# Entry of the even layer: norm weights by column, a projection of unscaled tokens, and an earlier state-space setup

## What is computed

```
x  = layer_norm(ALPHA*x + moe + ple, ln2_w, ln2_b)
hn = x * rsqrt(mean(x*x) + 1e-6) * norm_even_g      # rmsnorm
proj = hn @ w_in_even                               # q, k, v, u, z_a, z_b, 1024 columns each
# state-space model (s5) on u: per channel a complex recurrence
dt = exp(log_dt); mag = exp(lr*dt); ang = li*dt
a  = mag*(cos ang + i sin ang);  factors (a-1)/(lr+i li) scale B
x_t = a x_{t-1} + B u_t;  y_t = Re(C x_t) + D u_t   # run as phase turn, real scan, phase turn back
x  = x + concat(attention, glu(gelu(y))) @ w_out_even
```

## Time and profile before

| | us |
|---|---|
| median of three timed runs | 3200.54 |
| the profiled execution's own time | 3198.18 |
| its span | 3196.4 |
| PE busy | 3009.0 (94%) |
| DVE busy | 1547.4 (48%) |
| ACT busy | 837.8 (26%) |
| POOL busy | 283.5 (9%) |

### The profile page before, as it was taken

One profiled execution on the slowest core, in us unless ns is written; L12 is line 12 of the kernel. 1 busy time (PEld: TensorE's weight loads), 2 busy tenths in 40 slices (PEclk: granted clock), 3 DMA queues, 4 the chain that ended last, 5 costly groups with the idle time before them and its releaser, 6 DMA issues.

```text
span 3196.4 us, 42548 instructions
## 1 busy us (share of the span) xinstructions
PE 3009.0 (94%) x18244; PEld 2161.4 (68%) x18244; DVE 1547.4 (48%) x1846; ACT 837.8 (26%) x926; POOL 283.5 (9%) x260
## 2 busy tenths in 40 slices
PE   8999999899999999999999999879999998999898
PEld 6777777899977743333333333268858878998886
DVE  4465544674556522222222222357887554444765
ACT  3352221544434310110110110010000243444443
POOL 2042111000000000000000000035440000000100
PEclk9999988999998999999999999989999999999999
DMA  7543221446575599999999999843333355898543
GB/s 244 151 139 100 74 61 58 123 140 182 174 237 171 190 366 425 425 425 425 425 425 425 425 425 425 341 159 118 114 124 118 126 178 125 194 194 183 137 165 138
DMA packets 216144, 725.25 MB, mean 227 GB/s; under 512 B 16314, under 2 KB 18794, under 8 KB 165644
## 3 DMA queue, kind: packets, MB, share of 16 engines
q1 hardware_dynamic: 210716, 702.22, 62.6%
q0 software_dynamic: 4144, 18.14, 1.6%
q10 hardware_dynamic: 1088, 2.10, 0.2%
HBM read 720.28 MB, written 2.11 MB: 226 GB/s over the span
## 4 chain that ended last, share of the span: by engine, by line
PE 72%; DMA 12%; DVE 11%; ACT 4%; issue 1%; POOL 0%; DVEq 0%; ACTq 0%
PE psum L137 71%; DMA t<-in_w_up 12%; DVE t L283 8%; ACT t L254 2%; PE psum L143 2%; DVE t L294 1%; ACT t L256 1%; DVE t L298 1%; DVE t L306 0%; ACT L254 0%; POOL t L328 0%; DVE t L269 0%; ACT L256 0%; DMA t<-in_x 0%; DVE t L275 0%
## 5 line engine op out<-in xcount | busy, mean ns | idle before, releaser
L137 PE MATMUL psum<-t,t 128*128 128x256 f32 (+7 forms) x17166 | 2914.8, 379 | 135.3 <-DVE t L283 78.8
L137 PEld LDWEIGHTS psum<-t,t 128*128 128x128 f32 (+4 forms) x17166 | 2069.7, 175 | 941.2 <-issue 564.2
L283 DVE TENSOR_TENSOR t<-t,t 128x1024 fp32r<-128x1024 f32 (+6 forms) x642 | 786.0, 1224 | 495.8 <-ACT t L254 462.5
L254 ACT ACTIVATE t<-t 128x1024 fp32r<-128x1024 f32 (+8 forms) x521 | 528.6, 1015 | 901.4 <-PE psum L137 625.3
L283 DVE TENSOR_TENSOR t<-t,psum 128x1024 f32<-128x1024 f32 (+3 forms) x265 | 246.3, 929 | 741.3 <-PE psum L137 440.7
L254 ACT ACTIVATE t<-psum 128x1024 f32<-128x1024 f32 (+5 forms) x278 | 213.5, 768 | 1414.9 <-PE psum L137 1315.5
L328 POOL TENSOR_TENSOR t<-t,t 128x1024 f32<-128x1024 f32 (+8 forms) x133 | 222.9, 1676 | 571.7 <-DVE t L283 258.2
L283 DVE TENSOR_TENSOR t<-psum,t 128x1024 f32<-128x1024 f32 (+6 forms) x117 | 101.1, 864 | 121.9 <-PE psum L137 91.8
L143 PE MATMUL psum<-t,t 128*128 128x128 f32 (+1 forms) x566 | 87.9, 294 | 31.7 <-DVE t L294 18.0
L143 PEld LDWEIGHTS psum<-t,t 128*128 128x128 f32 (+1 forms) x566 | 67.6, 150 | 69.5 <-issue 39.8
L83 POOL DMA_DIRECT2D t<-in_s_lr x1 | 0.6, 574 | 1187.2 <-DVE t L306 1187.2
(11 more groups left out here) (67 smaller groups left out, 240.1 us busy)
## 6 DMA issues: line engine op xcount, KB each, us to landing
t<-in_w_gate SPq DMA_DIRECT2D x128, 1024.0 KB, 16.9
t<-in_w_up SPq DMA_DIRECT2D x128, 1024.0 KB, 18.4
t<-in_w_down SPq DMA_DIRECT2D x128, 1024.0 KB, 17.5
t<-in_w_in SPq DMA_DIRECT2D x160, 512.0 KB, 4.1
t<-in_w_in_odd SPq DMA_DIRECT2D x128, 512.0 KB, 5.4
t<-in_w_in_even SPq DMA_DIRECT2D x96, 512.0 KB, 3.8
t<-in_w_out SPq DMA_DIRECT2D x32, 512.0 KB, 4.3
t<-in_w_pg SPq DMA_DIRECT2D x32, 512.0 KB, 4.3
```

Of the source, the lines that this page charges most:

```text
L137: ins = self.e.matmul(o, l, r, start=start, stop=stop, skip_group_check=True)
L254: self.put(self.e.activation(o, i, f, scale=scale), event)
L283: self.put(self.e.tensor_tensor(o, a, b, op), event)
```

## The change

- **Norm by column.** DVE's second norm now only centres and scales each token (`centred`, one ts of 128x512 for each block and half, in place). Weight and bias are applied after PE's transposes, where a column is a partition: DVE (`gained`) writes `hTe` with weight and bias multiplied by the even gain (`l2g`), and ACT squares the same PSUM bank with weight and bias (`l2c`) into four buffers. Within a block DVE and ACT take turns on the two halves of the bank.
- **Unscaled projection.** PE starts u after half of the first block and puts the four sets of transposes between the pieces. POOL sums the squares (three tts of 128x1024, one of 128x512, one of 128x256), and PE forms `r1.sum` with one matmul after the eighth piece. DVE then makes the factor per token, scales u as it leaves PSUM (`states_in`, before a copy on ACT), and scales `hTe` in place, a quarter at a time, as soon as u has used it (`scaled_tokens`).
- **Earlier setup.** The small part of the state-space setup runs beside experts 8 to 10 on ACT and DVE; its loads (four DMAs) are issued in the experts too. After the meeting POOL has seven DMAs, then the powers, then the sum of squares, then the phases.
- **Residual rows later.** `x` gets `ln2_w` and `ln2_b` on POOL after phases 7: for each of two halves two broadcast loads of 512 KB, a wait, and four tts of 128x1024.
- **Layout and loads.** The experts' gather buffers move to the bottom of the memory so that six `w_in_even_2` pieces can land before the experts end; the two 1 MB loads of `ln2_w` and `ln2_b` on SP are gone.

The diff, cut to its core:

```diff
@@ tensor program, even()
+                def turned_pairs(j):
+                    w = pe.take("ev.T", j, of=(0, 3)).rearrange("p (k b t) -> p k b t", b=2, k=4)
+                    pe.wait_ge(("l2.x", j), j > 1 and ("ev.hTs", j - 2) or None)
+                    for k in range(4):
+                        for b in range(2):
+                            pe.tr(w[:, k, b, :], x[:, b, 512 * j + 128 * k:512 * j + 128 * k + 128],
+                                  event=("ev.T", j) if k == 3 and b else None)
+
+                turned_pairs(0)
+                for j in range(4):
+                    if j < 3:
+                        turned_pairs(j + 1)
+                    for i in (2 * j, 2 * j + 1):
+                        pe.wait_ge(("ev.hT", 2 * i + 1))
+                        some(first, 1)
+                ps = pe.take("r1.sum", of=(0, 3))
+                pe.wait_ge(("r1.squares",), ("ev.hTs", 3))
+                pe.mm(ps[:, 0:256], ones[:, 0:128], squares[0][:, 0, :], True, True, event=("r1.sum",))
                 some(first, 8)
-                rest = chain(native_b("ev.q", hTe, "w_in_even_2", 0, 1024, (0, 1)),
+
+                def queries():
+                    work = native_b("ev.q", hTe, "w_in_even_2", 0, 1024, (0, 1))
+                    for i in range(16):
+                        if i < 8:
+                            pe.wait_ge(("ev.hTn", i // 2))
+                        yield next(work)
@@ vector program: second_norm, the factor per token, the order
+
+                def centred(j):
                     for b in range(2):
-                        xc = x[:, b, cs]
-                        v.stt(xc, xc, mv[:, b, 0:1], l2w[:, cs], ALU.subtract, ALU.mult)
-                        v.stt(xc, xc, inv[:, b:b + 1], l2b[:, cs], ALU.mult, ALU.add, event=("l2.x", ci) if b else None)
-
-            def scaled_tokens():
-
-                v.wait_ge(("r1.sum", 3))
+                        xc = x[:, b, 512 * j:512 * j + 512]
+                        v.ts(xc, xc, mv[:, b, 0:1], inv[:, b:b + 1], ALU.subtract, ALU.mult,
+                             event=("l2.x", j) if b else None)
+
+                def gained(j):
+                    ps = v.bank("ev.T", j).rearrange("p (k b t) -> p k b t", b=2, k=4)
+                    v.wait_ge(("ev.T", j))
+                    for k in range(4):
+                        i = 4 * j + k
+                        if k == 2:
+                            v.wait_ge(("r1.square", j, 1))
+                        v.ts(hTe[:, i, :].rearrange("p (b t) -> p b t", b=2), ps[:, k], l2g[:, 0, i:i + 1],
+                             l2g[:, 1, i:i + 1], ALU.mult, ALU.add, event=("ev.hT", i))
+                    v.names(("ev.hTs", j))
+
+                centred(0)
+                centred(1)
+                v.wait_ge(("meet", "pe", 7), ("meet", "act", 7), ("meet", "pool", 7))
+                for j in range(4):
+                    gained(j)
+                    if j < 2:
+                        centred(j + 2)
...
+            def states_in(ci):
+                v.wait_ge(("ev.u", ci))
+                v.tt(uT[:, 4 * ci:4 * ci + 4, :], v.bank("ev.u", ci).rearrange("p (m t) -> p m t", m=4), over_tokens(4),
+                     ALU.mult, event=("ev.u.c", ci))
+                v.free("ev.u", ci)
+
+            def scaled_tokens(g4):
+                v.wait_ge(("used", "s", stream.turn + 9 + 2 * g4))
+                h4 = hTe[:, 4 * g4:4 * g4 + 4, :]
+                v.tt(h4, h4, over_tokens(4), ALU.mult, event=("ev.hTn", g4))
...
+                    if 8 <= ex < 11:
+                        (s5_decay, s5_angles, s5_factors)[ex - 8]()
...
                 s5_setup()
+                token_scales()
+                states_in(0)
+                for g4 in range(4):
+                    scaled_tokens(g4)
+                states_in(1)
                 s5()
@@ scalar program
+                    if ex == 8:
+                        a.wait_ge(("landed.s5a",))
+                        a.activation(dt, ld, ACT.Exp, event=("s5.dt",))
+                    elif ex == 9:
+                        a.wait_ge(("s5.lrdt",))
+                        a.activation(mag, mag, ACT.Exp, event=("s5.mag",))
+                    elif ex == 10:
+                        a.wait_ge(("s5.angles",))
+                        a.activation(sn, sn, ACT.Sin)
+                        a.activation(cs_, cs_, ACT.Sin, event=("s5.cos",))
...
+                ps = a.bank("ev.T", j).rearrange("p (k b t) -> p k b t", b=2, k=4)
+                a.wait_ge(("ev.T", j))
+                for k in (2, 3, 0, 1):
+                    i = 4 * j + k
+                    if k == 0:
+                        a.wait_ge(("ev.hT", i + 1))
+                    a.activation(squares[j][:, k, :].rearrange("p (b t) -> p b t", b=2), ps[:, k], ACT.Square,
+                                 bias=l2c[:, 1, i:i + 1], scale=l2c[:, 0, i:i + 1], event=("r1.square", j, k // 2))
                 a.free("ev.T", j)
@@ pool program
+            g.wait_ge(("mo.flagged",), ("pl.mul", 3))
+            g.load(("landed.s5a",), [(lr, I["s5_lr"]), (li, I["s5_li"]),
+                                     (ld[0:64, :], I["s5_ld"][0].partition_broadcast(64)),
+                                     (ld[64:128, :], I["s5_ld"][1].partition_broadcast(64))])
...
-            g.wait_ge(("s5.setup",))
+            g.wait_ge(("s5.factors",))
...
+            for j in range(1, 4):
+                g.wait_ge(("r1.square", 0, 0), ("r1.square", j, 0))
+                g.tt(squares[0], squares[0], squares[j], ALU.add)
+            g.tt(squares[0][:, 0:2], squares[0][:, 0:2], squares[0][:, 2:4], ALU.add)
+            g.tt(squares[0][:, 0], squares[0][:, 0], squares[0][:, 1], ALU.add, event=("r1.squares",))
+            g.wait_ge(("s5.setup",))
             make_phases(0)
             make_phases(1)
             for j in range(6):
                 make_phases(j + 2, ("s5.phased", j))
+            g.wait_ge(("s5.phases", 7))
+            for h in range(2):
+                ch = slice(1024 * h, 1024 * h + 1024)
+                g.load(("landed.l2", h), [(l2w, along("ln2_w")[:, ch]), (l2b, along("ln2_b")[:, ch])])
+                g.wait_ge(("landed.l2", h))
+                for b in range(2):
+                    g.tt(x[:, b, ch], x[:, b, ch], l2w, ALU.mult)
+                    g.tt(x[:, b, ch], x[:, b, ch], l2b, ALU.add, event=("l2.rest", h) if b else None)
+                g.wait_ge(("l2.rest", h))
@@ sync program
+            s.wait_ge(("mo.gu", 27))
+            pieces(stream, stream.turn, stream.turn + 4)
+            s.wait_ge(("mo.gu", 31))
+            pieces(stream, stream.turn + 4, stream.turn + 6)
```

More of the change, by code:

```diff
@@ L166, in __init__ @@
         self.raw, self.hi, self.lo = bufs
+        self.raw = [self.raw[(k - turn) % len(self.raw)] for k in range(len(self.raw))]
         self.known = known
@@ L530, in build @@
         scratch = at(bre_at, 1024)
+        early, b2 = phases[0][0].rearrange("p i t -> p (i t)"), phases[1][0].rearrange("p a t -> p (a t)")[:, 0:512]
+        b2 = b2.rearrange("p (i c) -> p i c", i=32)
         bw = at(8192, 4096).rearrange("p (h x) -> p h x", h=16)
+        l2w, l2b = [at(6144 + 1024 * k, 1024) for k in range(2)]
         top[0] = s5_at
@@ L1338, in tensor_program @@
             pe.stage("even")
[L1339 to L1347, removed]
             even()
@@ L1742, in scaled_tokens, with over_tokens @@
                 v.rcp(spread_row, spread_row)
-                for k in range(16):
-                    v.stt(hTe[:, k, :], hTe[:, k, :], gains[0][:, k:k + 1], spread_row, ALU.mult, ALU.mult,
-                          event=("ev.hT", k))
+            def over_tokens(n):
+                return spread_row.unsqueeze(1).broadcast_to([128, n, 256])
+            def states_in(ci):
[3 more added lines that the diff above has]
+                v.free("ev.u", ci)
@@ L1909, in scattered @@
                                     sums(v, 24 * b, 2 * c + h, b, 1024 * h + 512 * c)
+                v.wait_ge(("landed.gains",))
+                for k in range(2):
+                    v.tt(l2g[:, k, :], l2c[:, k, :], gains[0], ALU.mult)
                 for ex in range(34):
@@ L2029, in even @@
                 v.limit = 1 << 20
-                v.wait_ge(("s5.phases", 7))
+                v.wait_ge(("l2.rest", 1))
                 first = stream.first("w_out_even_2")
@@ L2643, in even @@
                 a.limit = 1 << 20
-                a.wait_ge(("ev.scored", 3), ("s5.phases", 7))
+                a.wait_ge(("ev.scored", 3), ("l2.rest", 1))
                 first = stream.first("w_out_even_2")
@@ L2761, in scalar_program @@
             for j in range(4):
-                ps = a.bank("ev.T", j).rearrange("p (b k t) -> p b k t", b=2, k=4)
-                a.wait_ge(("ev.T", j), j > 1 and ("r1.sum", j - 2) or None)
-                a.activation(squares[j % 2].rearrange("p (k b t) -> p b k t", k=4, b=2), ps, ACT.Square,
-                             event=("r1.square", j))
```

(4 more changed lines are left out.)

93 lines of the change are left out of this document (42 added, 51 removed).

## The result

The changed kernel takes 3201.40 us, the median of 20 runs (3196.63 to 3205.79), the kernel before 3197.20 in 20 runs beside them (3190.48 to 3202.13). The medians differ by 4.2 us; the ratio is 1.0014, with a 95% interval of 1.0008 to 1.0020: 4.5 us slower (2.6 to 6.4). That is clear of zero and yet within the 0.2% (6.4 us) that the prediction set as no change. The three runs first shown for the kernel before lie 3.3 us above its 20, so only the difference is to be compared: +5.3 was forecast, +4.5 measured. The profiled execution of the changed kernel took 3199.03 us (span 3197.2), that of before 3198.18 (3196.4).

What follows compares the result with a forecast made beforehand. DVE's chain was taken to bound the entry until u starts, PE from 2182.59 to 2456. Entry -1.5 and residual rows +6.8 gave +5.3 on the profiled 3198.18, 3203.5; with 2.4 for the median 3205.8 us, range 3193.5 to 3211.0.

Steps and rivals of the forecast that it cites:

- step 1: Entry, second norm: DVE's two-pointer ts take 0.5 us, PE's first transposes start at 2088.0 instead of 2090.17.
- step 3: Entry, POOL's queue: DMAs to 2087.5, powers 30.7 us, sum of squares 8.4 us, done at 2126.7 if undisturbed.
- step 4: Entry: DVE's blocks 2 and 3 (2.0 us) and setup (up to 4.8) delay POOL's sum to 2133.4; PE idles almost 11.
- the slower rival: Entry: pad clearing and first blocks also hold POOL up, sum at 2137.6, entry loses 2.7, 3210.0 us; chance 0.12.
- The rival with an undisturbed POOL: Entry: POOL is not held up, PE waits 4 us instead of 11, a gain of 8.2; chance 0.14.
- steps 5 to 7: Second half of u to 2164.4, a 3.5 us wait behind it, then group 0 without its 2.26 us wait, to 2182.8.
- Gain of the entry: Shift of PE's start on group 1's transposes: 1.5 us gained, ends from 8.2 gained to 2.7 lost.
- Residual rows: Group 6's scans lose 8.3 us beside POOL's tts; PE waits 4.4 at `b_times_u(7)`, clock 2.4: cost 6.8 us.
- The second pair: Second pair of residual-row loads, from about 2415: covered by 8.4 us of DVE idle time in group 7.
- Setup and SP at nothing: Setup moved into the experts and SP's loads cost nothing; without the experts' cover the setup costs at most 7.7 us.
- If the end of the experts moves: Sign in the profile after that would show the prediction wrong; it expected the experts' period unchanged.

Runs made afterwards that it cites:

- second trace of the changed kernel: The changed kernel measured again without any edit: 3200.07 us, ratio 1.0008 to the kernel before.
- setup later: Changed kernel with DVE's six setup tts moved behind `states_in(0)`: 3201.25 us, ratio 1.0017 to the kernel before.
- the sum first: Changed kernel with POOL's sum of squares moved between the near and the far powers: 3191.49 us, ratio 0.9980 to the kernel before.
- the turn early: Changed kernel with group 0's copies right behind the setup and B transposed two pieces before u's end: 3194.58 us, ratio 0.9996 to before.

## Why the prediction was right

The sum, -1.5 + 6.8 = +5.3 us, was measured as +4.5 (1.0008 to 1.0020 is 2.6 to 6.4). The traces split it into -3.75 + 7.90 for the one and, in the second trace of the changed kernel, -3.76 + 6.0. So both terms have the right sign and mechanism, but the entry gained 2.2 us more than worked out, and the rows cost 1.1 more in one trace and 0.8 less in the other. That the total came within a microsecond is in part luck: in the trace that was shown first the two errors cancel (+4.15), in the other they do not (+2.2, and 1.0008 in its runs). By its steps:

- **Centring (step 1).** The first transposes start at +4.92, worked out as 4.8. A ts with two pointers takes 0.57 on average, not 0.5, against 0.43 with constants.
- **POOL's work (step 3).** DMAs at +4.3 as worked out. The powers without the setup beside them are 31.9 us and not 30.7, the sum 9.6 and not 8.4: three tts of 2.34 instead of 2.07, and longer gaps.
- **Disturbance (step 4): the mis-sized term.** "POOL loses up to 4.8" to the setup, and 2.0 to blocks 2 and 3. The runs showed 2.1 for the setup (setup later), and not over 1.2 for the rest, the difference of 31.9 and 30.7. The model, in which POOL loses the length of every such DVE instruction, charges double beside POOL's short tts. The pads' memsets, on which the slower rival stood, cost nothing: POOL's four 128x32 tts beside them take 1.36 us, as elsewhere. So 3.3 us of the 6.8 charged were there. The 1.2 us that the sum of squares took longer hid part of this: the ninth piece came at +48.1 instead of +50.2, and the wait was 10.2 instead of 11. The rival with an undisturbed POOL said 4 us of wait; with the setup out of the way 8.05 were measured, so that rival was wrong by POOL's own time, too.
- **Second half, wait behind u, group 0 (steps 5 to 7).** From the ninth piece to group 1's transposes 49.3 us, worked out as 49.4. The wait behind u was 3.56 us, worked out as 3.5.
- **Gain of the entry.** 3.75 us instead of 1.5: the 2.2 us come from step 4, 3.5 less disturbance against 1.2 more for the sum.
- **Residual rows.** Eight scans 8.05 us longer, put at 8.3; PE's wait 4.16 and 4.08, put at 4.4; what is left of the 7.90 and 6.0, for the clock, 2.2 and 1.9, put at 2.4. The second pair, which the prediction held covered by idle time of DVE, was not covered in the trace shown first, where it stretched six tts by 8.15 us (a wait of 1.57); in the other it stretched them by 6.1 and cost no wait.
- **Setup and SP at nothing.** The experts' stretch is unchanged, with the six table loads foreseen. "If the end of the experts moves" was a sign of being wrong; it moved by 4.5 us, but with the start of the experts, and so does that of one kernel from run to run.

On the scans, had only tts beside POOL. The Trainium skill (SBUF — State Buffer, Who interferes with whom) states the rule for DVE instructions with two SBUF inputs in general; this case's trace agrees for scans: 13.82 and 13.74 us beside POOL's tts, 5.77 without. The same section speaks of a lock for a whole instruction; by that, POOL should lose the 4.4 us of the setup's tts, and the measured 2.1 is less (2.2 with the sum first). Where the rest goes no run here shows.

## What to carry to other kernels

When the first consumer is made independent of a norm, follow the norm's factor along the engine that now makes it. Here 17.6 us were won at the start of u and lost again, because the sum that PE needs after eight pieces stood behind 34 us of other work on POOL's queue, and changes of order alone (the sum first, the turn early) gave 17.4 us back at group 1.

Optional work on an engine that holds another one up has a price given by its place: the same eight tts cost 6 to 8 us beside DVE's scans on the path and nothing 90 us later. And a wait that is removed uncovers the next: an early sum lengthened the four copies, a late setup too, and only edits made together carried their gain to the end.

## What the runs showed of the hardware that was not expected

- DVE's scans (two on-chip inputs) wait beside POOL's tts as tts do: one beside each of POOL's four 128x1024 tts takes 2.66 to 2.84 us instead of 0.69.
- What DVE loses in a meeting depends on the length of POOL's instructions; what POOL loses hardly did. Beside POOL's short tts of the powers (128x32 and 128x64) DVE's six 128x512 tts take 4.43 us against 4.32 alone (setup later, 2129.38), and POOL loses 2.1. Beside its sum of squares, in the kernel with the sum first, they take 7.96. POOL's five tts of the sum and the six of 128x32 behind them take 13.7 us there (2103.85 to 2117.59) and 11.5 where nothing is beside them, so it loses 2.2.
- A POOL tt of 128x1024 takes 2.34 us on plain tiles with DVE idle (three in the sum of squares), and 2.44 in the residual rows beside the attention (eight), against 2.07 for those of the phases in the kernel before, whose operands are broadcast in part. Whether the pattern or the operation is the reason was not tried.
- A DVE ts with two pointer scalars takes 0.55 to 0.60 us at 128x512 (0.57 on average of eight) and 0.54 at 128x256 from PSUM, where one with constants takes 0.43 and 0.42.
